# One-hots of the gate spread, token by token on VectorE

## The reference, cut to what matters

```python
    expert = i1 * PEER_KEYS + i2              # PEER_KEYS = 128
    gate = jax.nn.softmax(best_v, axis=-1)
    ...
        u = u_emb[e_blk]
        a = jnp.einsum('bthkd,btd->bthk', u, h_blk).astype(jnp.float32)
        act = (jax.nn.gelu(a) * g_blk).astype(h_blk.dtype)
        return jnp.einsum('bthk,bthkd->btd', act, v_emb[e_blk])
```

## Time and profile before

| | |
|---|---|
| median of 3 runs | 5172.26 us (5167.73 to 5175.76) |
| span of the profiled execution | 5167.3 us; the page gives no other time of it |
| mean granted TensorE clock | 0.963 of full speed |
| PE, DVE, ACT, POOL busy | 93%, 59%, 32%, 33% of the span |
| spread phase | from 2640 us to 3708 us of the span |

### The profile page before, as it was taken

How to read it: one execution, slowest core, us unless ns; L and a number is a source line. 1 busy time by engine, 2 the same in 40 slices (tenths; PEclk the granted TensorE clock), 3 DMA queues, 4 the chain that set the end, 5 groups by cost and what they waited for, 6 DMA issues and landing times. The chain is left out here.

```text
span 5167.3 us, 66578 instructions
## 1 busy us (share of the span) xinstructions
PE 4813.1 (93%) x23440; PEld 3844.4 (74%) x23440; DVE 3059.9 (59%) x4062; ACT 1628.0 (32%) x2577; POOL 1713.3 (33%) x818
## 2 busy tenths in 40 slices
PE   6999999967989979999979999999799999999998
PEld 5666666635767758888868888888688888888886
DVE  3777777775423336465578888888544444444444
ACT  2555555553422322222233333332211111111111
POOL 1444444331223112121136666666422222222221
PEclk8999999978999989999989999999899999999999
DMA  2111111104432122222224444444553333434441
GB/s 75 41 44 40 45 46 46 37 25 159 154 122 74 73 87 85 71 89 79 70 90 138 146 146 146 146 144 142 193 193 142 143 142 142 144 146 146 146 143 60
DMA packets 259768, 555.72 MB, mean 108 GB/s; under 512 B 15536, under 2 KB 146864, under 8 KB 257456
## 3 DMA queue, kind: packets, MB, share of 16 engines
q1 hardware_dynamic: 259632, 554.01, 31.1%
HBM read 384.60 MB, written 169.35 MB: 107 GB/s over the span
## 5 line engine op out<-in xcount | busy, mean ns | idle before, releaser
L148 PE MATMUL expert_o<-expert_ahi,expert_vhi 128*128 128x512 f32 x2048 | 798.6, 390 | 34.4 <-POOL expert_vlo L2000 30.0
L150 PE MATMUL expert_o<-expert_ahi,expert_vlo 128*128 128x512 f32 x2048 | 798.1, 390 | 0.0
L149 PE MATMUL expert_o<-expert_alo,expert_vhi 128*128 128x512 f32 x2048 | 798.1, 390 | 0.0
L2052 DVE TENSOR_TENSOR expert_acc<-expert_acc,expert_o 128x512 f32<-128x512 f32 x512 | 352.1, 688 | 736.4 <-PE expert_o L150 732.4
L1386 POOL TENSOR_TENSOR ulo<-uraw,uhi 128x1024 fp32r<-128x1024 f32 x128 | 447.0, 3493 | 770.4 <-ACT uhi L1382 769.6
L2000 POOL TENSOR_TENSOR expert_vlo<-expert_vraw,expert_vhi 128x1024 fp32r<-128x1024 f32 x128 | 323.4, 2527 | 1053.7 <-ACT expert_vhi L2018 1053.7
L148 PE MATMUL spread_a<-hhi,uhi 128*128 128x512 f32 x1280 | 505.7, 395 | 15.1 <-POOL ulo L1386 15.1
L150 PE MATMUL spread_a<-hhi,ulo 128*128 128x512 f32 x1280 | 499.7, 390 | 0.0
L149 PE MATMUL spread_a<-hlo,uhi 128*128 128x512 f32 x1280 | 498.8, 390 | 0.0
L1869 DVE TENSOR_TENSOR spread_gate<-spread_eq,spread_parts 128x2048 bf16<-128x2048 bf16 x128 | 485.1, 3831 | 9.1
L148 PEld LDWEIGHTS expert_o<-expert_ahi,expert_vhi 128*128 128x128 f32 x2048 | 385.2, 188 | 115.9 <-issue 36.2
(11 more groups left out here) (289 smaller groups left out, 9165.8 us busy)
## 6 DMA issues: line engine op xcount, KB each, us to landing
uraw<-in_peer_u SPq DMA_DIRECT2D x128, 512.0 KB, 4.0
gelu_u<-ugelu SPq DMA_DIRECT2D x128, 512.0 KB, 2.9
gates<-spread_stage SPq DMA_DIRECT2D x16, 4096.0 KB, 17.6
expert_act<-gelu_u SPq DMA_DIRECT2D x128, 512.0 KB, 3.6
expert_graw<-gates SPq DMA_DIRECT2D x128, 512.0 KB, 4.4
expert_vraw<-in_peer_v SPq DMA_DIRECT2D x128, 512.0 KB, 6.4
mix_w_raw<-in_w_mix SPq DMA_DIRECT2D x56, 512.0 KB, 3.6
xattn_w_raw<-in_w_cross SPq DMA_DIRECT2D x32, 512.0 KB, 3.5
```

Source lines behind the costliest of these rows:

```text
L148: nc.tensor.matmul(out, whi, xhi, start=(first and i == 0), stop=False)
L149: nc.tensor.matmul(out, whi, xlo, start=False, stop=False)
L150: mm = nc.tensor.matmul(out, wlo, xhi, start=False, stop=(last and i == len(terms) - 1))
L2052: nc.vector.tensor_tensor(acc[:, k, h * H:h * H + H], acc[:, k, h * H:h * H + H], ops[:, d, h], ALU.add).then_inc(added, 1)
```

## The change

The instruction over 16 tokens that reads `parts` by broadcast is replaced by instructions over one token, which take i1, i2 and the gate part as scalars per partition. Such a scalar is read from a float32 tile `scal`, which VectorE fills by a copy at each step. A `tensor_scalar` then does the compare (for `one1`), or the compare and the multiply (for the three parts of `gate`). GpSimd no longer takes part in it. `eq` and its semaphores go. VectorE signals every 4 tokens, and TensorE waits for its bank alone.

```diff
-        eq = m.sb("eq", [P, B, KEYS], BF16)
+        scal = m.sb("scal", [P, 2, 5, B])
...
-                pool.wait_ge(eq_made, n + 1)
-                pool.wait_ge(g_done, n * NB + NB)
-                nc.gpsimd.tensor_tensor(gate[:, 2, b], eq[:], parts[:, 4, ds(n * B, B)].unsqueeze(2).to_broadcast([P, B, KEYS]),
-                                        ALU.mult).then_inc(pool_gated, 1)
                 ex.split_low(pool, tile + 1, 1 - b)
...
                 dve.wait_ge(g_done, n * NB + NB)
-                one_hot(one1[:, b], 0, n).then_inc(one1_made, 1)
-                dve.wait_ge(pool_gated, n + 2)
-                dve.wait_ge(dve_gated, n * 2 + 4)
-                one_hot(eq[:], 1, n).then_inc(eq_made, 1)
-                dve.wait_ge(eq_made, n + 1)
-                for i in range(2):
-                    nc.vector.tensor_tensor(gate[:, i, b], eq[:],
-                                            parts[:, 2 + i, ds(n * B, B)].unsqueeze(2).to_broadcast([P, B, KEYS]),
-                                            ALU.mult).then_inc(dve_gated, 1)
+                nc.vector.tensor_copy(scal[:, b], parts[:, :, ds(n * B, B)]).then_inc(scal_made, 1)
+                dve.wait_ge(scal_made, n + 1)
+                for t in range(B):
+                    nc.vector.tensor_scalar(one1[:, b, t], iota[:], scal[:, b, 0, t:t + 1], None, ALU.is_equal)
+                    for i in range(3):
+                        ins = nc.vector.tensor_scalar(gate[:, i, b, t], iota[:], scal[:, b, 1, t:t + 1],
+                                                      scal[:, b, 2 + i, t:t + 1], ALU.is_equal, ALU.mult)
+                    if t % 4 == 3:
+                        ins.then_inc(spread_made, 1)
...
                 ex.product(pe, tile, b)
-                pe.wait_ge(one1_made, n + 1)
-                pe.wait_ge(dve_gated, n * 2 + 6)
-                pe.wait_ge(pool_gated, n + 3)
                 for bank in range(NB):
+                    pe.wait_ge(spread_made, n * NB + (bank + 1))
                     pe.wait_ge(staged, n * NB + (bank + 1))
```

More of the change, by code:

```diff
@@ L1777, in spread_phase @@
         part_made, rest_made = m.sem("part_made"), m.sem("rest_made")
-        eq_made = m.sem("eq_made")
-        one1_made = m.sem("one1_made")
-        dve_gated, pool_gated = m.sem("dve_gated", start=4), m.sem("pool_gated", start=2)
+        scal_made = m.sem("scal_made")
+        spread_made = m.sem("spread_made")
         g_done = m.sem("g_done", start=2 * NB)
```

## The result

The changed kernel takes 5202.05 us (median, 5199.08 to 5206.81) against 5174.01 for the kernel before in the same runs. The ratio is 1.0062, 95% interval 1.0050 to 1.0074: slower by 28 us. The profiled execution spans 5200.2 us, 32.9 more than before.

What follows compares the result with a forecast made beforehand. TensorE bounds the kernel, with VectorE hidden under its 13.67 us steps; 5.9 us gained in the first step, plus 3.6 of later waits, less up to 2, gives 7 to 9: 5172.3 - 7.3 = 5165, range 5156 to 5245.

Steps and rivals of the forecast that it cites:

- rival B: Spread stage, slower: two scalars fetched one after the other, each GpSimd split stops VectorE; +22 us, 5195, centre 5205; chance 0.35.
- the price of the second scalar: VectorE's compare-and-multiply: two scalars cost between 0.061 us (fetched together, the value taken) and 0.17.
- the other case: VectorE's 48 compare-and-multiply instructions per step with two scalars at 2 x 0.061: 0.226 us each, a step of 13.8.
- L545's leftover of 0.17: VectorE's one row with two scalars: 0.17 us left for both scalars and for a wait on GpSimd inside it.
- The cap on the gain: Spread stage: the most a faster VectorE can give is 13.3 + 2.3 = 15.6 us, 0.3%.
- the fixed 0.069: Each short VectorE instruction: 0.069 us from start to start that does not depend on its elements.
- The copy: VectorE's copy of 80 elements at each step: taken as 0.35 us, could be 0.6 at no consequence.
- The stop: GpSimd's split of 2.39 us could stop VectorE for some 2.3 us, ten times per tile, 23 us.
- 16.4 us per step before it is the bound: VectorE in the spread stage: stays hidden up to 131.0 / 8 = 16.4 us per step, catching up in the two extras.
- C: VectorE's compares don't get the fast rate: 20.1 us a step, stage ends 251 us later, 5423; chance 0.09.
- D: Faster by over 0.2%: the first step loses its clock drop too, nearly all 15.6 us come, 5160 or less; chance 0.09.
- The first step: Start of the spread stage: TensorE ends the first spread at about 2662 in place of 2667.9, 5.9 us gained.

Runs made afterwards that it cites:

- The third multiply alone: The kernel before, with only GpSimd's third multiply given to VectorE in the old form over 2048 elements; 5168.02 us, ratio 0.9997.

## Why the prediction was wrong

It forecast no measurable change (5165) and gave 0.35 to what happened, rival B, whose own sum was 5195 and whose centre was 5205; measured are 5202. The range held the time, the forecast did not.

**What failed** is one step, the price of the second scalar: "I take fetched together, as the row leaves room for a wait". The two scalars cost 0.06 each: instructions are 0.223 apart, where I took 0.165 and had 0.226 for the other case. L545's leftover of 0.17 would then be 0.12 for two scalars and some 0.05 for GpSimd's hold, an estimate. The row allowed both, and I took the value at the edge of its bounds instead of the one that repeats the price of the first scalar. On 3072 instructions the step is 178 us of VectorE, 2.8 per step of 16 tokens. The forecast's 10.9 lay 2.6 below the 13.5 from which rival B decides. With one scalar, which is what the forecast had priced, the same kernel takes 0.9984 of the time before: 8 us less, where the forecast had 7.

**What held.** The cap on the gain (15.6 us), which no kernel here broke, and the loss without a cap. The 0.061 for a scalar (0.223 less 0.163). The sum of the fixed 0.069, one scalar and the data of 0.035: 0.163 to 0.165 measured for 0.165. No run measures the fixed part and the data apart at 128 elements, but the 0.53 for 384 elements at 1.04 ns fits the same 0.069. The data is the four elements per cycle of the Trainium skill, "VectorE: DVE Perf Modes", section "The perf-mode tier table"; the trace agrees, since 0.163 less 0.069 and 0.061 leaves 0.033. The copy took 0.22 and its user began 0.26 after its start, under my 0.35. The stop: 2.2 us against my 2.3, read from L545, where it showed as a sum that stood still. The section "Who interferes with whom" of the Trainium skill's "SBUF — State Buffer" says that of GpSimd and VectorE in a two-port mode the one that comes first keeps the shared ports for its whole instruction; the trace agrees with all three lengths, as far as GpSimd coming first goes. With splits of 0.46, 2.38 and twice 2.4 us VectorE was stopped for 0.25, 2.2 and 4.3, and the long splits were not stretched by it.

**What rival B got right for a partly wrong reason.** It gave +22 for the phase, which grew by 37.8. It let VectorE work without a pause. It idles 41.5 us, since with two buffers it can't use all of the 21.6 us of extras. The bound per step that I gave, "16.4 us per step before it is the bound", was too kind for the same reason: 15.7 already lost. The sum was saved by a step of 13.6, not 13.8, by stops that take some 160 us in all, not 175 (VectorE's chain from 2650.7 to its last one-hot at 3722.3, less 64 x 13.6 and the idle 41.5), and by the 6 us between the phases that nobody had counted. That its centre of 5205 is 3 us from the measured time is luck.

**Rivals C and D.** The compares do run at the fast rate. D's gain of over 0.2% was not reached by any kernel here; the lowest ratios are 0.9982 to 0.9984.

**The first step** was to gain 7 to 9 us; in the changed kernel its four waits are 4.16, 2.09, 1.86 and 1.86, 10.0 us in all, about the 9.7 of before, as a split stopped VectorE twice in it. With one scalar TensorE's wait in the whole phase was 7.5 us.

## What to carry to other kernels

Price a short instruction by its distance to the next, and price each scalar per partition in it: at 128 elements the fixed part and two scalars were 0.19 us of 0.223, and the data only 0.033 (at the 0.133 of the old compare a step would have been some 20 us, as in rival C). If a row leaves two values for such a term and it is multiplied by thousands, the forecast belongs to the value that repeats a measured one, and the likeliest case must be built on it.

Before giving VectorE single-source instructions at their fast rate, look for long GpSimd instructions beside them, and count each as a stop of nearly its whole length on VectorE's chain (2.2 us for 2.38 here); then compare with the slack per step and with how far the buffers let VectorE run ahead.

## What the runs showed that I had not expected

In the kernel before, GpSimd's split beside the old two-tensor instructions was stretched too (2.39 to 4.44). Beside the new ones it ran at its own pace (2.38), and VectorE alone paid, about 2.2 us either way. The form is not all of it: in "The third multiply alone" the split began 1.2 us before a two-tensor compare, kept its 2.39 us, and VectorE paid 1.1. What decides who is slowed was not tested.

Moving work to VectorE made VectorE's round shorter: five two-tensor instructions with half a split beside them took 12.4 us, where four and GpSimd's multiply took 14.66.
